# Row gathers placed between an oct's own chunks, gate rows applied oct by oct, and separate banks for the last oct

## The reference

```
g_idx   = argmax(t @ w_gr + b_gr)                     # 1 of 4 groups per row
top_v, top_i = top_k(e_logits of that group, 2)       # 2 of its 8 experts
dense_w = softmax(top_v) * group weight               # one weight per row and expert
hid = silu(t @ w_gate[e]) * (t @ w_up[e]) * dense_w   # 32 experts, hidden width 256
moe = sum over e of hid @ w_down[e]
x   = layer_norm(ALPHA * x + gate2 * moe)
```

## Time and profile before

| | before |
|---|---|
| median of 3 runs | 1084.74 us (1083.73 to 1085.54) |
| profiled execution | 1089.13 us, span 1087.2 us |
| mean granted clock of TensorE | 0.947 |
| busy share of the span: PE, PEld, DVE, ACT, POOL | 87%, 48%, 50%, 31%, 8% |
| share of the span on the chain that ended last | PE 73%, DVE 12%, DMA 9%, issue 3%, ACT 2% |
| HBM read, rate over the span | 298.93 MB, 280 GB/s |

### The profile page before, as it was taken

The page is one execution under the profiler, slowest core; times in us unless marked ns, Lnnn a source line. Parts: engine busy times, 40 slices in busy tenths (PEclk is TensorE's granted clock), DMA queues, the critical chain, the costliest instruction groups (busy, mean ns, idle before and its releaser), DMA issues.

```text
span 1087.2 us, 15034 instructions
## 1 busy us (share of the span) xinstructions
PE 946.6 (87%) x5770; PEld 519.4 (48%) x5770; DVE 540.2 (50%) x1247; ACT 340.9 (31%) x725; POOL 91.3 (8%) x90
## 2 busy tenths in 40 slices
PE   3899998999869889999869998799949899989982
PEld 1475676554535434353226667564445434344321
DVE  5524315785563342423666344495674242523548
ACT  2211012461313424342331213263223433324331
POOL 0150000101300000000016000000310000000000
PEclk9999999999869999999997999999969999999987
DMA  9978999403487899999937124013198699999961
GB/s 319 365 302 341 421 385 379 188 20 155 190 338 311 346 420 412 422 411 421 418 113 265 52 80 158 16 43 111 64 382 365 231 422 420 396 421 383 422 253 61
DMA packets 47507, 305.03 MB, mean 281 GB/s; under 512 B 5971, under 2 KB 6228, under 8 KB 14644
## 3 DMA queue, kind: packets, MB, share of 16 engines
q1 hardware_dynamic: 40524, 275.67, 62.7%
q0 software_dynamic: 6208, 26.06, 6.7%
q10 hardware_dynamic: 688, 2.17, 0.7%
HBM read 298.93 MB, written 4.95 MB: 280 GB/s over the span
## 4 chain that ended last, share of the span: by engine, by line
PE 73%; DVE 12%; DMA 9%; issue 3%; ACT 2%; SPq 1%; ACTq 0%; DVEq 0%
PE bank L1049 18%; PE bank L937 8%; PE bank L1028 7%; DMA ring<-in_moe_gate_up 6%; PE bank L771 6%; PE bank L750 4%; PE bank L1137 4%; PE bank L679 4%; PE bank L782 3%; DMA ring<-in_w_mod 2%; PE bank L880 2%; PE bank L647 2%; PE bank L823 2%; PE bank L661 2%; PE bank L812 1%
## 5 line engine op out<-in xcount | busy, mean ns | idle before, releaser
L937 PE MATMUL bank<-ring,act_t 128*128 128x512 f32 x192 | 84.1, 594 | 0.0
L1049 PE MATMUL bank<-ring,arena 128*32 128x512 f32 x480 | 60.9, 626 | 24.9 <-DMA ring<-in_moe_gate_up 13.6
L1028 PE MATMUL bank<-sel,h_hi 128*128 128x384 f32 x192 | 70.3, 366 | 9.4 <-DVE sel L2068 9.4
L1484 ACT ACTIVATE arena<-bank 128x384 f32<-128x384 f32 x64 | 31.5, 491 | 129.0 <-PE bank L1028 129.0
L1137 PE MATMUL bank<-y_hi,selT 128*128 128x512 f32 x144 | 63.0, 438 | 7.1 <-DVE y_lo L2130 6.7
L1028 PE MATMUL bank<-sel,h_lo 128*128 128x384 f32 x192 | 67.0, 349 | 0.0
L2130 DVE SCALAR_TENSOR_TENSOR y_lo<-bank,region_v,y_hi 128x512 fp32r<-128x512 f32 x48 | 34.6, 748 | 53.0 <-ACT y_hi L1506 53.0
L1137 PE MATMUL bank<-y_lo,selT 128*128 128x512 f32 x144 | 57.6, 400 | 0.0
L937 PEld LDWEIGHTS bank<-ring,act_t 128*128 128x128 f32 x192 | 35.8, 190 | 43.6 <-issue 43.6
L1137 PEld LDWEIGHTS bank<-y_hi,selT 128*128 128x128 f32 x144 | 27.8, 193 | 53.5 <-DVE y_lo L2130 28.4
L771 PE MATMUL bank<-act_t,ring 128*128 128x384 f32 x160 | 52.3, 487 | 0.0
(11 more groups left out here) (351 smaller groups left out, 1741.5 us busy)
## 6 DMA issues: line engine op xcount, KB each, us to landing
ring<-in_moe_gate_up SPq DMA_DIRECT2D x60, 1024.0 KB, 9.7
region_k<-in_moe_gate_up SPq DMA_DIRECT2D x40, 1024.0 KB, 9.1
ring<-in_w_mod SPq DMA_DIRECT2D x33, 1024.0 KB, 9.2
ring<-in_moe_down SPq DMA_DIRECT2D x32, 1024.0 KB, 10.5
arena<-in_moe_down SPq DMA_DIRECT2D x28, 1024.0 KB, 9.6
arena<-in_moe_gate_up SPq DMA_DIRECT2D x16, 1024.0 KB, 11.4
ring<-in_w_in SPq DMA_DIRECT2D x9, 1024.0 KB, 13.0
ring<-in_w_out SPq DMA_DIRECT2D x8, 1024.0 KB, 5.2
```

What stands on the lines that cost most here:

```text
L937: mm = pe.matmul(ps[2 * t + half][:, :], act_t[:, 2 * c + k, t * P:(t + 1) * P], w[:, k, half * 512:(half + 1) * 512], start=(c == 0 and k ...
L1028: mm = pe.matmul(ps[gather_bank(o, k)][:, 0:TOK], src[:, t, k * P:(k + 1) * P], sel[:, t, :, :].rearrange("p v n -> p (v n)"), start=(t == ...
L1049: return pe.matmul(out[r, :], stationary[:, r], moving, start=start, stop=stop, tile_position=(0, UNIT * j), skip_group_check=True)
L1484: act.activation(xg[:, first:first + VISITS, k, :], ps[gather_bank(o, k)][:, 0:TOK].rearrange("p (v n) -> p v n", n=P), ACT.Copy)\
```

## The change

Three things are changed.

- The gathers of an oct are moved. Gathers 0 and 1 come between chunks 6 and 7 of the oct before; gather 2 after chunk 0 of their own oct, 3 and 4 after chunk 1, 5 (`HELD`) after chunk 3, 6 and 7 between the two down chunks of the second half. `gathered` moves alike on ScalarE, and on VectorE `pick` of the next oct now waits for all gathers of this one. Gathers 5 to 7 use banks that hold the sums of the oct before, so gather 5 waits for the first half of these and the second half's first scatter waits until all eight banks are copied.
- The gate row and the residual are applied in every oct: `gated` multiplies a bank by the gate row into `moe`, `added` adds that to x (in oct 0 to ALPHA * x). `folded` and `residual` are gone. In the last oct the second half goes tile by tile, with the statistics of a tile right behind its last add.
- The last oct has a bank and a `y_hi`, `y_lo` buffer for each of its six blocks (bank 5 twice), and `down_visit` multiplies both down chunks of a half for one visit before the next visit begins. GpSimd waits for the last scatter before it loads `dft` for the next layer, since the new buffers lie in that memory.

```diff
+LAST_BANKS = (4, 5, 0, 1, 2, 5)
+HELD = 5
+    y_hi_last = nc.alloc_sbuf_tensor_at("y_hi_last", [P, BLOCKS, 512], F32R, offset=arena_at + 4 * X_AT)
...
             if l > 0:
+                pool.wait_ge(e["sct"], SCATTERED * OCTS * l)
                 pool.dma_start(dft, a["dft"]).then_inc(s["dft_in"], 16)
...  gather
+                if o > 0 and k == HELD:
+                    pe.wait_ge(e["acc"], SUMS * (OCTS * l + o - 1) + TT)
...  place_weights
-                        pe.wait_ge(e["x_out"], K8 * (OCTS * l + o + 1))
+                        pe.wait_ge(e["x_out"], K8 * (OCTS * l + o) + HELD)
...
+            def down_visit(o, half, v):
+                pe.wait_ge(e["hd_out"], 2 * (OCTS * l + o + 1))
+                y_free(o, VISITS * half + v)
+                for k in range(2):
+                    c = CHUNK_AT["D", o, 2 * half + k]
+                    landed(c)
+                    for j in range(UNITS):
+                        mm = tile(y_bank(o, VISITS * half + v), hdT[2 * v + k], weights(c)[:, 2 * j + v, :], j, k == 0, k == 1)
+                mm.then_inc(e["done"], 1)
...  scatter
+                if i == VISITS and o + 1 < OCTS:
+                    pe.wait_ge(e["x_out"], K8 * (OCTS * l + o + 2))
...  order on TensorE
-            for k in range(2, K8):
-                gather(1, k)
             for o in range(1, OCTS):
                 gate_up(o, 0)
-                place_weights(o, 0)
+                gather(o, 2)
                 gate_up(o, 1)
+                gather(o, 3)
+                gather(o, 4)
                 turns(o - 1)
                 choices(o - 1, 0)
+                place_weights(o, 0)
...
                 gate_up(o, 3)
+                gather(o, 5)
                 down(o - 1, 2)
+                gather(o, 6)
+                gather(o, 7)
                 down(o - 1, 3)
...
                 gate_up(o, 5)
-                ahead(0, 1)
                 gate_up(o, 6)
-                ahead(2, 3, 4)
+                if o + 1 < OCTS:
+                    gather(o + 1, 0)
+                    gather(o + 1, 1)
                 gate_up(o, 7)
-                ahead(5, 6, 7)
             turns(last)
             choices(last, 0)
-            down(last, 0)
+            down_visit(last, 0, 0)
             choices(last, 1)
-            down(last, 1)
+            down_visit(last, 0, 1)
+            down_over(last, 0)
             scatter(last, 0)
-            down_over(last, 0)
             scatter(last, 1)
             scatter(last, 2)
-            down(last, 2)
-            down(last, 3)
+            down_visit(last, 1, 0)
+            down_visit(last, 1, 1)
...  VectorE
+            def gated(o, half, t):
+                dve.wait_ge(e["sct"], SCATTERED * (OCTS * l + o) + 5 * half + VISITS + t)
+                dve.tensor_tensor(moe[:, t, cols], ps[SUM_BANKS[t]][:, :], gates[:, min(t, 1), cols], ALU.mult).then_inc(e["acc"], 1)
+            def added(o, half, t):
+                dve.wait_ge(e["acc"], SUMS * (OCTS * l + o) + TT * half + t + 1)
+                if o == 0:
+                    link(dve.scalar_tensor_tensor(x[:, t, cols], x[:, t, cols], ALPHA, moe[:, t, cols], ALU.mult, ALU.add))
+                else:
+                    link(dve.tensor_tensor(x[:, t, cols], x[:, t, cols], moe[:, t, cols], ALU.add))
...  order on VectorE, an oct
                 summed(o - 1, 0)
                 copy(c + 5)
+                rows_added(o - 1, 0)
+                copy(c + 6)
+                copy(c + 7)
                 if o + 1 < OCTS:
+                    dve.wait_ge(e["x_raw"], K8 * (OCTS * l + o + 1))
                     pick(o + 1, (0,))
...
                 copy(c + 9)
-                if o == OCTS - 1:
-                    folded(0)
+                rows_added(o - 1, 1)
                 copy(c + 10)
...  order on VectorE, last oct
+                copy(c + 3)
                 summed(last_oct, 0)
-                copy(c + 3)
                 y_rest(last_oct, 3)
                 y_rest(last_oct, 4)
-                for t in range(TT):
-                    residual(t, 0)
+                added(last_oct, 0, 0)
+                added(last_oct, 0, 1)
                 y_rest(last_oct, 5)
+                added(last_oct, 0, 2)
                 for t in range(TT):
                     link(half_stats(t, 0))
-                summed(last_oct, 1)
                 for t in range(TT):
-                    residual(t, 1)
+                    gated(last_oct, 1, t)
+                    if tiles_whole:
+                        added(last_oct, 1, t)
+                        statistics(t)
```

More of the change, by code:

```diff
@@ L381, in at, with y_bank, y_high_of, y_low_of @@
         return l * PER[name] + (PER[name] if i is None else i)
+    def y_bank(o, i):
+        return ps[LAST_BANKS[i] if o == OCTS - 1 else 4 + i % 2]
+    def y_high_of(o, i):
+        return y_hi_last[:, i, :] if o == OCTS - 1 else y_hi[:, i % 2, :]
+    def y_low_of(o, i):
+        return y_lo_last[:, i, :] if o == OCTS - 1 else y_lo[:, i % 2, :]
     h_dram = nc.dram_tensor("h_hi_rows", (DEPTH, P, TT * D), F32, kind="Internal").ap()
@@ L1122, in down_over @@
                     for j in range(UNITS):
-                        mm = tile(ps[4 + n % 2], hdT[4 + k], stage[c % 2][:, j, :], j, k == 0, k == 1)
+                        mm = tile(y_bank(o, VISITS * half + 2), hdT[4 + k], stage[c % 2][:, j, :], j, k == 0, k == 1)
                     mm.then_inc(e["over"], 1)
@@ L1135, in scatter @@
                         pe.wait_ge(e["acc"], SUMS * (OCTS * l + o) + t + 1)
-                    for j, y in enumerate((y_hi, y_lo)):
-                        mm = pe.matmul(ps[SUM_BANKS[t]][:, :], selT[:, v, t * P:(t + 1) * P], y[:, n % 2, :], start=(v == 0 and j == 0),
+                    for j, y in enumerate((y_high_of(o, i), y_low_of(o, i))):
+                        mm = pe.matmul(ps[SUM_BANKS[t]][:, :], selT[:, v, t * P:(t + 1) * P], y, start=(v == 0 and j == 0),
                                        stop=(v == 2 and j == 1), skip_group_check=True)
@@ L1164, in _ @@
             gate_up(0, K8 - 1)
-            for k in range(2, K8):
-                gather(1, k)
             for o in range(1, OCTS):
-                def ahead(*pieces):
-                    if o + 1 < OCTS:
-                        for k in pieces:
-                            gather(o + 1, k)
                 gate_up(o, 0)
-                place_weights(o, 0)
+                gather(o, 2)
                 gate_up(o, 1)
+                gather(o, 3)
+                gather(o, 4)
                 turns(o - 1)
                 choices(o - 1, 0)
+                place_weights(o, 0)
                 place_weights(o, 1)
@@ L1547, in _ @@
             copy(K8 - 1)
-            for k in range(2, K8):
-                gathered(1, k)
             for o in range(1, OCTS):
                 c = CHUNK_AT["G", o, 0]
-                def ahead(*pieces):
-                    if o + 1 < OCTS:
-                        for k in pieces:
-                            gathered(o + 1, k)
                 silu(o - 1)
                 copy(c)
+                gathered(o, 2)
                 copy(c + 1)
+                gathered(o, 3)
+                gathered(o, 4)
                 turned(o - 1)
@@ L1569, in _ @@
                     copy(c + n)
+                for k in range(HELD, K8):
+                    gathered(o, k)
                 y_high(o - 1, 3)
@@ L1574, in _ @@
                 copy(c + 9)
-                ahead(0, 1)
                 copy(c + 10)
-                ahead(2, 3, 4)
+                if o + 1 < OCTS:
+                    gathered(o + 1, 0)
+                    gathered(o + 1, 1)
                 copy(c + 11)
-                ahead(5, 6, 7)
             last_oct, c = OCTS - 1, len(CHUNKS) - 4
@@ L1584, in _ @@
             copy(c + 1)
-            for i in range(3):
-                y_high(last_oct, i)
+            y_high(last_oct, 0)
+            y_high(last_oct, 1)
             copy(c + 2)
+            y_high(last_oct, 2)
             copy(c + 3)
@@ L2129, in y_rest @@
                 weight = COL_AT + VISITS * (o % 2) + i % VISITS
-                dve.scalar_tensor_tensor(y_lo[:, n % 2, :], ps[4 + n % 2][:, :], rt[:, weight:weight + 1], y_hi[:, n % 2, :].bitcast(F32),
+                dve.scalar_tensor_tensor(y_low_of(o, i), y_bank(o, i)[:, :], rt[:, weight:weight + 1], y_high_of(o, i).bitcast(F32),
                                          ALU.mult, ALU.subtract).then_inc(e["y_low"], 1)
@@ L2151, in folded @@
+            def summed(o, half):
+                if o == 0:
                     dve.wait_ge(s["gate_in"], 32 * (2 * l + 2))
                     dve.wait_ge(s["x1"], at("x1", l))
-                link(dve.tensor_tensor(moe[:, t, :], moe[:, t, :], gates[:, min(t, 1), :], ALU.mult))
-                link(dve.scalar_tensor_tensor(x[:, t, :], x[:, t, :], ALPHA, moe[:, t, :], ALU.mult, ALU.add))
-            def residual(t, half):
-                cols = slice(half * 512, (half + 1) * 512)
```

(11 more changed lines are left out.)

68 lines of the change are left out of this document (26 added, 42 removed).

## The result

The changed kernel takes 1067.12 us (median of 4 runs, 1065.41 to 1071.81) where the kernel before took 1085.14 beside it, 18.0 us less by the medians. The ratio on record is 0.986, 95% interval 0.9816 to 0.9904, which is 15 us less (10 to 20). The forecast was 1062.7, -22.0, with a range of 1053 to 1078: the sign and the range held; of the gain 4.0 us did not come by the medians, 7 by the ratio. The profiled execution took 1067.81 us, span 1066.0, mean granted clock 0.945.

The account below looks back on a forecast made before the run. The prediction took the experts to be bound by the weight stream, with holes made by TensorE's bunched gathers. 14.4 us (stream) plus 7.6 (last oct) gave 22.0 off the median 1084.74, so 1062.7 us, range 1053 to 1078.

Parts of the forecast that it names:

- What bounds the kernel, and the hole: Experts, bound by the weight stream: bunched gathers make holes in it; moving them closes these, worth 14.4 us.
- 14.4 us for the stream: Weight stream in both layers without holes: 5.9 us gained in layer 0 and 8.5 in layer 1.
- 4.9 and 4.7: Gain in us from closing the hole behind the block of six gathers, layer 0 and layer 1.
- 1.0 and 3.85: Gain in us in the later octs, chunk 16 to 40, layer 0 and layer 1, against 119.8 for 24 chunks.
- Gates by oct at nothing: VectorE's adds into x in every earlier oct cost 0, with 2 us a layer as the bad end.
- The last oct: From chunk 40's wait to the last scatter and norm: 5.3 + 6.4 - 2.1 - 2.0 = 7.6 us gained, from 3 to 13.
- so I charge 1.0 us a layer: Last oct: cost of TensorE's clock falling behind the longer new wait; 0 if it stays up, 1.7 at half speed.
- The walk without this term, 45.3: Last oct timed step by step in the new order: last scatter 45.3 us after chunk 40's wait, against 50.6 and 51.7.
- The norm: Behind the last scatter: one more add behind the last y_lo, so 0.9 and 1.2 us subtracted for the two layers.
- The sum: Whole kernel: 14.4 us for the stream plus 7.6 for the last oct, 22.0 us faster.
- Faster by the stream alone: Rival: the last oct waits for landings twice, at half clock, and gives back its gain; 1070.3 us, chance 0.16.
- Slower by the clock: Rival: spread waits leave TensorE at half rate for a share of every oct; 1092 us, chance 0.05.

Follow-up runs that it names:

- e1: The kernel before with the moved gathers alone, gates and last oct as before: 1070.34 us, ratio 0.9874.
- e3: The changed kernel with the last oct's old order and two buffers, gathers and gates by oct as changed: 1069.05 us, ratio 0.9888.
- e4: The changed kernel with 24 unread matmuls on TensorE over the last oct's wait for chunks 44 and 45: 1059.78 us, ratio 0.9801.
- e6: The changed kernel with the first half's adds and half statistics ahead of the second half's last y_lo on VectorE: 1065.13 us, ratio 0.9846.
- e7: The changed kernel with oct 1's first two gathers behind oct 0's last gate-up chunk instead of ahead of it: 1068.02 us, ratio 0.989.

## Why the prediction was nearly right

- **What bounds the kernel, and the hole.** Right. Without the 2.24 us of the earlier start, oct 1's first gate-up would stand at 350.75 (348.51 in the profile; 350.7 was predicted) and SP's issue at 353.04 (353). The shares are 1.01 to 1.02 in every stretch that was short. Of 14.4 us for the stream 12.9 came: 3.3 and 2.8 up to chunk 16 (384.51 and 878.14 now) for 4.9 and 4.7, then 1.3 and 5.4 for 1.0 and 3.85. TensorE comes to chunk 40 of layer 0 without a wait (504.02), so there its own order and no longer the stream is last.
- **Gates by oct at nothing.** Not contradicted: they cost nothing that can be told, and may have given up to 3.5 us of the stream's gain (e1 to e3). The wait of 1.88 us for the gated rows is 0.26 now.
- **The last oct.** The step that failed is "so I charge 1.0 us a layer" for the clock. The direction was right, the size was not: it cost 2.6 us in layer 0 and 3.8 in layer 1 (47.4 and 49.3 here against 44.8 and 45.4 in e4), 6.4 instead of 2.0, and more than the 1.7 a layer that was allowed for. Two things were wrong in the term. A visit was put at 1.0 us; its 16 matmuls take 1.74 at full clock (541.00 to 542.74), so nearly twice as much work stood at half clock. And the rows of layer 0 show one chunk of 16 matmuls at half (3.38 us), with the next at full (1.92 us at 538.95), but layer 1 of the same execution, which none of the forecast's rows shows there, has both at half behind the same wait of 1.88 us:

```profile
1036.75 1.36 PE L1082 MATMUL bank<-cst,act_t 128*128 128x128 f32 x6 [1.88 <-DVE act_t L2106]
...
1038.97 3.64 PE L1049 MATMUL bank<-ring,region_w 128*32 128x512 f32 x16
...
1043.48 3.64 PE L1049 MATMUL bank<-region_k,region_w 128*32 128x512 f32 x16
```

In the changed kernel the clock stayed down from the wait into the overflow, about 10 us, with a second wait in between. The walk without this term, 45.3, is near what e4 measures (44.8 and 45.4), but in part by luck: the second half's two visits took 3.6 us there (534.38 to 537.97) where the walk had 2.0, and the 2.2 us of waits that it put around them, for chunk 47 and for `y_lo`, did not come. What the piece up to the last scatter gave is 5.6 us where 5.3 + 6.4 - 2.0 = 9.7 was forecast.
- **The norm.** 0.9 and 1.2 were taken off; layer 0 gained 0.6, layer 1 lost 0.9, together 1.8 better than forecast. Behind the last `y_lo` stand one add (0.68 us) and the three half statistics (2.15), which stood there before too. e6, which takes all of them away from there, gains 2.0, so the greater part of that gain is the half statistics and not the extra add.
- **The sum.** 22.0 less 1.5 (stream), less 4.1 (last oct), plus 1.8 (norm) is the 18.2 of the pieces.
- **The rivals.** "Faster by the stream alone" put 1070.3; with the last oct at half clock the kernel came within 3.2 us of it; e1, which has the gathers alone, took 1070.34. "Slower by the clock" did not come: of the changed kernel's stretches of 10 us from 350 to 500 and from 840 to 990 all are at 1.00 but one at 0.83 (480 to 490). The waits that kept the full clock before are in the earlier trace rows, not in the earlier trace rows: 1.92 us for 16 matmuls behind 2.30 and 1.95 us.

## What to carry to other kernels

A block of work that stands ahead of the multiplication which frees a load's slot makes a hole in the stream: look for two issues that are further apart than a load lasts, and put the block behind the multiplication, at a place where the next slots have time to spare: e7's two gathers only delayed the next load. A reorder that trades two short waits for one longer one has to be priced with everything that runs behind that wait at half clock. Whether the clock falls can differ between two passes through the same wait, so look at every pass in the trace before pricing it. If nothing else fits in the wait, unread matmuls do.

## What the runs showed of the hardware

A wait's length alone does not tell whether the clock falls. After 1.80 us the visit's matmuls took 1.93 instead of 1.06; after 2.10 us, in layer 1 of the changed kernel, a gate-up chunk kept its 1.92:

```profile
976.51 1.92 PE L1068 MATMUL bank<-ring,arena 128*32 128x512 f32 x16 [2.10 <-DMA ring<-in_moe_gate_up]
```

Ahead of the first, TensorE had waited 0.26 us for the transposes (522.11) and then done 1.7 us of small matmuls; ahead of the second it had gone from chunk to chunk and gather to gather, busy 9.41 of 10 us in the stretch from 965 to 975. But what TensorE did in the 20 us before the wait does not tell it either. In e1 it waits 1.88 us in both layers, 20.7 us after chunk 40 and behind the same matmuls; the two down chunks behind the wait ran at half clock (the first for most of its time) in layer 0 and at full in layer 1:

```profile
524.21 1.01 PE L1085 MATMUL bank<-cst,act_t 128*128 128x128 f32 x6 [1.88 <-DVE act_t L2106]
...
525.84 3.08 PE L1052 MATMUL bank<-ring,region_w 128*32 128x512 f32 x16
...
529.78 3.64 PE L1052 MATMUL bank<-region_k,region_w 128*32 128x512 f32 x16
...
1022.48 1.01 PE L1085 MATMUL bank<-cst,act_t 128*128 128x128 f32 x6 [1.88 <-DVE act_t L2106]
...
1024.12 1.92 PE L1052 MATMUL bank<-ring,region_w 128*32 128x512 f32 x16
...
1026.51 1.92 PE L1052 MATMUL bank<-region_k,region_w 128*32 128x512 f32 x16
```

From chunk 40 to the last scatter's end that is 50.6 us against 47.3. I did not expect the stream to be untouched by TensorE: 420 to 424 GB/s in stretches where TensorE was busy 10.00 of 10 us.
